# Preparing an SSM's tables with 32 products and expanded input matrices, and turning x inside two weight units

## What is computed

```
u, sq, sk, sv, dq, dk, dv, gate_logits = split(rmsnorm(x) @ w_in[l])
lam_bar = exp(lam * dt);  b_bar = ((lam_bar - 1) / lam) * bmat          # 32 groups, 64 states, 16 channels
states  = scan(lam_bar, b_bar @ u);  y = Re(c @ states) + d_skip * u
y_ssm = glu(gelu(y));  y_sb = stick_breaking(sq, sk, sv)
y_da  = rmsnorm(differential(rope(dq), rope(dk), dv), diff_subln)
x += (sum_n sigmoid(gate_n) * (branch_n @ w_branch_n)) @ w_out
x += cross_attention(rmsnorm(x), rmsnorm(mem)) @ w_xo
x += square(relu(rmsnorm(x) @ w_up)) @ w_down
```

## Time and profile before

| | |
|---|---|
| median of 3 runs (lowest to highest) | 1056.09 us (1056.09 to 1057.02) |
| the profiled execution | 1055.7 us, span 1054.0 us |
| mean granted clock | 0.988 |
| PE / DVE / ACT busy | 96% / 73% / 53% of the span |
| HBM traffic | 166 GB/s over the span |

### The profile page before, as it was taken

How to read it: one execution, slowest core, us unless ns; L and a number is a source line. 1 busy time by engine, 2 the same in 40 slices (tenths; PEclk the granted TensorE clock), 3 DMA queues, 4 the chain that set the end, 5 groups by cost and what they waited for, 6 DMA issues and landing times. The chain is left out here.

```text
span 1054.0 us, 19160 instructions
## 1 busy us (share of the span) xinstructions
PE 1009.7 (96%) x7544; PEld 895.4 (85%) x7544; DVE 765.8 (73%) x1176; ACT 563.0 (53%) x879; POOL 45.1 (4%) x100
## 2 busy tenths in 40 slices
PE   6979999999999999999989999999999989999996
PEld 6967899989897888888889779998998878888885
DVE  5958997788865766888845559877787658656664
ACT  7456535467555645444454554354657556444443
POOL 5001100000000004000000030000000000000000
PEclk9989999999999999999989999999999999999999
DMA  8625436545543555656535643364555435556561
GB/s 331 196 90 141 137 119 207 196 141 180 183 158 120 188 194 180 190 190 187 192 102 177 169 156 121 121 193 128 179 181 162 151 128 180 190 190 189 191 188 72
DMA packets 58281, 176.22 MB, mean 167 GB/s; under 512 B 14416, under 2 KB 16464, under 8 KB 58064
## 3 DMA queue, kind: packets, MB, share of 16 engines
q1 hardware_dynamic: 58048, 174.99, 52.0%
q10 hardware_dynamic: 144, 0.00, 0.0%
HBM read 171.82 MB, written 3.15 MB: 166 GB/s over the span
## 5 line engine op out<-in xcount | busy, mean ns | idle before, releaser
L1241 DVE TENSOR_TENSOR s_w_lo<-s_raw,s_w_hi 128x1024 fp32r<-128x1024 f32 x312 | 375.3, 1231 | 92.0 <-ACT s_w_hi L865 88.3
L865 ACT ACTIVATE s_w_hi<-s_raw 128x1024 fp32r<-128x1024 f32 x312 | 319.8, 1053 | 174.4 <-PE p_T L1800 73.0
L1798 PE MATMUL p_T<-s_hT,s_w_hi 128*128 128x256 f32 x576 | 166.1, 288 | 1.1 <-issue 0.6
L1799 PE MATMUL p_T<-s_hT,s_w_hi 128*128 128x256 f32 x576 | 162.9, 283 | 0.0
L1800 PE MATMUL p_T<-s_hT,s_w_lo 128*128 128x256 f32 x576 | 162.9, 283 | 0.0
L1798 PE MATMUL p_A<-s_w_hi,s_bT_hi 128*128 128x512 f32 x320 | 125.1, 391 | 2.3 <-DVE s_bT_lo L1241 2.3
L1800 PE MATMUL p_A<-s_w_hi,s_bT_lo 128*128 128x512 f32 x320 | 124.8, 390 | 0.0
L1799 PE MATMUL p_A<-s_w_lo,s_bT_hi 128*128 128x512 f32 x320 | 124.6, 389 | 0.0
L1798 PEld LDWEIGHTS p_T<-s_hT,s_w_hi 128*128 128x128 f32 x576 | 110.3, 191 | 5.2 <-issue 2.7
L1799 PEld LDWEIGHTS p_T<-s_hT,s_w_hi 128*128 128x128 f32 x576 | 110.4, 192 | 0.1
L1800 PEld LDWEIGHTS p_T<-s_hT,s_w_lo 128*128 128x128 f32 x576 | 110.3, 192 | 0.0
(11 more groups left out here) (268 smaller groups left out, 1906.8 us busy)
## 6 DMA issues: line engine op xcount, KB each, us to landing
s_raw<-in_weights SPq DMA_DIRECT2D x312, 512.0 KB, 3.5
s_x<-in_x SPq DMA_DIRECT2D x1, 1024.0 KB, 10.6
s_dv<-in_ssm_bc SPq DMA_DIRECT2D x2, 512.0 KB, 8.9
u_turn<-s_st_y SPq DMA_DIRECT2D x4, 256.0 KB, 4.9
s_uB<-u_turn SPq DMA_DIRECT2D x16, 64.0 KB, 4.0
s_bt<-in_mem SPq DMA_DIRECT2D x1, 1024.0 KB, 7.0
s_mem_t<-in_mem_t SPq DMA_DIRECT2D x1, 1024.0 KB, 9.0
y_turn<-s_st_y SPq DMA_DIRECT2D x16, 64.0 KB, 2.2
```

Of the source, the lines that this page charges most:

```text
L865: return nc.scalar.activation(o, i, f, **kw)
L1241: return V.tensor_tensor(o, i0, i1, op)
L1798: mm(o, lhi, rhi, start=first, stop=False, **kw)
L1799: mm(o, lhi, rlo, start=False, stop=False, **kw)
```

## The change

The tables are made in another way. `bN0` becomes block-diagonal over the two groups of a tile, so `mm_k` is 32 matmuls of 128 rows by 32 columns into one bank; DVE takes them out with two operations (`p_k`), adds `diag_d` there, and SP spreads them by way of DRAM into `kt` (4 + 8 DMAs, `spread_k`). `bt` is loaded already expanded by channel (`load_b`, 1 MB per layer, a new input), the powers are transposed by two small matmuls (`mm_f`), copied by ACT (`p_f`), sent through DRAM into `bF` (2 + 8 DMAs, `turn_f`), and DVE multiplies the two in place in six operations (`p_bt`); `mm_bt`, `p_bv` and their copies are gone. `p_ph` moves to units 7 and 8, `p_bt` takes units 9 to 11; `da_o` 0, `da_c` 1 and `da_n` 1 move from unit 25 to 26. The two turns of x for the MLP move into the middle of units 45 and 46, and ACT and DVE take the norm in two parts; both prepare weights early from unit 44 on. `xa_p` takes the first half of memory for all four heads and then the second. Several inputs of units are awaited by halves. In `p_b0`, `diag_d` shrinks from two operations of 64 x 512 to one of 128 x 64, with four tiny ones once. In side stages, `t` is the layer whose tables are made.

```diff
-MIDWAY = []
+K_AT = [22, 25]
+F_AT = [15, 18, 2 * (AT_UNIT["up", 0, 0] + 13) + 11, 2 * (AT_UNIT["up", 0, 0] + 13) + 14]
+MIDWAY = [("turn_x", "mlp", 0), ("turn_x", "mlp", 1)]
...
-        after(-1, "mm_bt", 1, 0)
...
-        for r in range(2):
-            after(u["bv"][r], "p_bv", tgt, r)
+        after(u["f"][0], "mm_f", tgt)
+        after(u["f"][1], "p_f", tgt)
+        for n in range(3):
+            after(u["bt"][n], "p_bt", tgt, n)
...
-        pre(0, dict(ct=-1, cv=(3, 4), b0=5, bv=(7, 8), ph=(9, 10, 11)))
-        blocks((6, 6, 7), ((9, 9), (9, 9), (10, 10), (10, 10)))
+        pre(0, dict(ct=-1, f=(2, 3), cv=(3, 4), b0=5, ph=(7, 7, 8), bt=(9, 10, 11)))
+        after(6, "mm_k", 0)
+        after(7, "p_k", 0)
...
-        pre(1, dict(ct=up0 + 12, cv=(up0 + 13, up0 + 16), b0=up0 + 17, bv=(up0 + 20, up0 + 21),
-                    ph=(up0 + 24, up0 + 25, up0 + 28)))
+        pre(1, dict(ct=up0 + 9, f=(up0 + 13, up0 + 13), cv=(up0 + 12, up0 + 13), b0=up0 + 16,
+                    ph=(up0 + 17, up0 + 20, up0 + 21), bt=(up0 + 24, up0 + 25, up0 + 28)))
     else:
-        blocks((None, 0, 1), ((None, 0), (3, 3), (4, 4), (5, 5)))
+        after(0, "p_k", 1)
...
-    after(25, "da_o", 0)
-    after(25, "da_c", 1)
-    after(25, "da_n", 1)
+    after(26, "da_o", 0)
+    after(26, "da_c", 1)
+    after(26, "da_n", 1)
     after(27, "da_o", 1)
...
     after(AT_UNIT["xo", 0], "stats", "mlp", 0)
-    after(AT_UNIT["xo", 1], "turn_x", "mlp", 0)
+    after(AT_UNIT["xo", 0], "turn_x", "mlp", 0)
+    after(AT_UNIT["xo", 0], "norm", "mlp", 0)
     after(AT_UNIT["xo", 1], "turn_x", "mlp", 1)
-    after(AT_UNIT["xo", 1], "norm", "mlp")
+    after(AT_UNIT["xo", 1], "norm", "mlp", 1)
     after(AT_UNIT["xo", 1], "stats", "mlp", 1)
...
-ACT_PREP_EARLY = set(range(0, 16)) | set(range(AT_UNIT["up", 0, 0], NU))
-DVE_PREP_EARLY = set(range(0, 6)) | set(range(AT_UNIT["up", 0, 0], NU))
+ACT_PREP_EARLY = set(range(0, 16)) | set(range(AT_UNIT["xo", 0], NU))
+DVE_PREP_EARLY = set(range(0, 6)) | set(range(AT_UNIT["xo", 0], NU))
...
+            def load_b(t):
+                load(bt[:, :, :, :], a["ssm_bt"][t], bt_landed)
+
+            def turn_f(t, part, st):
+
+                if part == 0:
+                    sp.wait_ge(*st.at(*freed(0, "X0", ("mm_f", t))))
...
+                        load(dst[r], fT[PC * r:PC * r + PC, :], f_out)
+                else:
+                    sp.wait_ge(*st.at(f_out, 2 * (t + 1)))
+                    src = f_turn[t].rearrange("(n k) (h s) -> h n k s", n=BL, h=2)
+                    for h in range(2):
+                        for j in range(BL):
+                            p = PC * h + GC * j
+                            load(bF[p:p + GC].rearrange("p r (i s) -> p (r i) s", s=STATES),
+                                 src[h, j].unsqueeze(0).broadcast_to([GC, 2 * STILES, STATES]), f_in)
+
+            def spread_k(l, part, st):
+
+                if part == 0:
+                    use = ("mm_k", l)
+                    sp.wait_ge(*st.at(*freed(l, stage_banks(use)[0], use)))
+                    dst = k_turn[l].rearrange("p (m q) n -> q p m n", q=4)
+                    for q in range(4):
+                        load(dst[q], kst[32 * q:32 * q + 32, :, :], k_out)
+                else:
+                    sp.wait_ge(*st.at(k_out, 4))
+                    for h in range(2):
+                        for j in range(BL):
+                            p = PC * h + GC * j
+                            load(kt[p:p + GC, :, GC * j:PC], k_turn[l][GC * h:GC * h + GC, :, 0:PC - GC * j], k_in)
...
+                    if l == 0 and c in F_AT:
+                        turn_f(F_AT.index(c) // 2, F_AT.index(c) % 2, st)
+                    if c in K_AT:
+                        spread_k(l, K_AT.index(c), st)
...
+                        for h in range(2):
+                            rows, c = slice(PC * h, PC * h + PC), slice(GC * h, GC * h + GC)
+                            tt(bN0[rows, r, :, c].unsqueeze(1), q[0][rows], q[1][rows], ALU.add if r else ALU.subtract)\
+                                .then_inc(*st.mid())
...
+                def p_k(t):
+
+                    use = ("mm_k", t)
+                    b = stage_banks(use)[0]
+                    src = bank[b][:, 0:BL * PC].rearrange("p (m c) -> p m c", c=PC)
+                    dve.wait_ge(*st.at(*full_at(l, b, use)))
+                    V.tensor_copy(kst[:, :, GC:PC], src[:, :, GC:PC]).then_inc(*st.mid())
+                    tt(kst[:, :, 0:GC], src[:, :, 0:GC], diag_d, ALU.add).then_inc(*st.sig(*freed(l, b, use)))
+
+                def p_bt(t, n):
+
+                    if n == 0:
+                        dve.wait_ge(*st.at(bt_landed, t + 1))
+                        dve.wait_ge(*st.at(f_in, 2 * BL * (t + 1)))
+                        for i in range(2):
+                            tt(st_y[:, i, :], bT[:, i], bF[:, i]).then_inc(*st.mid())
+                    elif n == 1:
+                        for i in range(2):
+                            tt(bF[:, 1 - i], bT[:, i], bF[:, 1 - i]).then_inc(*st.mid())
+                    else:
+                        tt(bT[:, 0], st_y[:, 0, :], st_y[:, 1, :], ALU.subtract).then_inc(*st.mid())
+                        tt(bT[:, 1], bF[:, 0], bF[:, 1], ALU.add).then_inc(*st.sig(bt_ready))
...
-                def inputs(key):
+                def inputs(key, half):
 
                     if key == ("glu", 1):
-                        return [(gelu_ready, 2)]
+                        return [(gelu_ready, half + 1)]
...
-                        return [(glu_ready, 2)]
-                    if key == ("wout", 0):
-                        return [(mg_ready, 2)]
-                    if key == ("wout", 1):
-                        return [(mg_ready, 4)]
+                        return [(glu_ready, half + 1)]
+                    if key in (("wout", 0), ("wout", 1)):
+                        return [(mg_ready, 2 * key[1] + half + 1)]
...
-                        return [freed(l, stage_banks(("xa_p", h))[0], ("xa_p", h)) for h in (2, 3)]
+                        return [freed(l, stage_banks(("xa_p", h))[0], ("xa_p", h)) for h in (2 * half, 2 * half + 1)]
                     if key[0] == "down" and key[2] == 0:
-                        return [(hid_ready, 2 * key[1] + 2)]
+                        return [(hid_ready, 2 * key[1] + half + 1)]
...
+                    elif kind == "mm_f":
+                        t = s[1]
+                        pe.wait_ge(*st.at(pow_ready, t + 1))
+                        pe.wait_ge(*st.at(*before(l, "X0", s)))
+                        for r, rows in enumerate(HALVES):
+                            ins = mm(bank["X0"][rows, 0:P], FACTORS[:, r, 3:3 + BL, :].rearrange("p n i -> p (n i)"),
+                                     ident[:, :], start=True, stop=True, skip_group_check=True)
+                        ins.then_inc(*st.sig(full["X0"]))
                     elif kind == "mm_k":
                         t = s[1]
+                        b = stage_banks(s)[0]
                         pe.wait_ge(*st.at(ct_ready, 2 * (t + 1)))
                         pe.wait_ge(*st.at(b0_ready, t + 1))
-                        for b in stage_banks(s):
-                            pe.wait_ge(*st.at(*before(l, b, s)))
-                        tiles = [(bank[b][32 * q:32 * q + 32, :], rows, q)
-                                 for b, rows in zip(stage_banks(s), HALVES) for q in range(4)]
-                        for m in range(STILES // 4):
+                        pe.wait_ge(*st.at(*before(l, b, s)))
+                        for m in range(BL):
                             for r in range(2):
-                                for o, rows, q in tiles:
-                                    mm(o[:, PC * m:PC * m + PC], bN0[rows, r, 4 * m + q, GC:3 * GC],
-                                       ct[rows, r, 4 * m + q, :], start=(r == 0), stop=False, skip_group_check=True)
...
+                                for q in range(4):
+                                    ins = mm(bank[b][32 * q:32 * q + 32, PC * m:PC * m + PC], bN0[:, r, 4 * m + q, :],
+                                             ct[:, r, 4 * m + q, :], start=(r == 0), stop=(r == 1), skip_group_check=True)
                         ins.then_inc(*st.sig(full[b]))
...
-                    elif kind == "xa_p":
...
-                        pe.wait_ge(*st.at(*before(l, b, s)))
+                    elif kind == "xa_p" and s[1] == 0:
                         for mt in range(2):
-                            ins = mm(bank[b][:, 0:T], vN[:, mt, h * P:h * P + P], eT_b[h][:, mt, :],
-                                     start=(mt == 0), stop=(mt == 1))
-                        ins.then_inc(*st.sig(full[b]))
+                            pe.wait_ge(*st.at(*freed(l, f"T{mt}", ("xv", 0))))
+                            for h in range(XA_HEADS):
+                                b, tb = stage_banks(("xa_p", h))[0], stage_banks(("xa_t", h))[0]
+                                if mt == 0:
```

(55 more changed lines are left out.)

81 lines of the change are left out of this document (27 added, 54 removed).

## The result

The changed kernel takes 1060.34 us (median of 6 runs, 1058.96 to 1062.59), the kernel before in the same session 1056.45 us. The ratio is 1.0034 with a 95% interval of 1.0022 to 1.0045: slower by 0.34%, outside the range that was forecast, and on the other side. The profiled span grew from 1054.0 to 1059.1 us, so 5.1 us are to be explained.

A forecast was written before the change was run, and what follows sets the result against it. PE, busy 96% of the span, was taken to bound the kernel, its idle time paid again through low clock. Terms summed to -7.8 us: 1047.9 against the profiled 1055.7, 1048.3 against the median; range 1038 to 1056.

The forecast's parts named there:

- Behind unit 26 a chain starts: Units 26 to 28: moved ACT and DVE stages take 9.65 us, `da_o` 1 waits 3.1; +5.14 a layer, +10.3 in all.
- rival C: Behind unit 26: two more ACT table loads of 1.28 us on the chain, +2.56 a layer, 1053.4 us; chance 0.11.
- At nothing: Loads and DMAs of `load_b`, `spread_k`, `turn_f`, and half-wise waits at branch, wout and down: no cost where PE doesn't wait.
- DVE in layer 0: Layer 0's table units: 2.1 us of new PE stalls at `sb_u` behind `nl`, 0.6 of an old wait gone; +1.5.
- Rival D: Layer 0, units 7 to 13: DVE becomes the bound and the stretch doesn't shrink, 1058.3 us; chance 0.08.
- mm_k: Layer 0 behind unit 6: 64 records take 2.0 us, saving 5.9; unit 7's low clock gives 0.7 back; -6.6.
- Start of layer 1: Before unit 0: it starts at 533.8 behind DVE's sum of x, -7.4, less 1.4 for low clock; -6.0.
- mm_bt: Its runs between units disappear: -4.2 us in layer 0, -3.5 in layer 1.
- xa_p: Before unit 44: products start at V's first half, unit 44 needs only heads 0 and 1; -2.0 a layer, -4.1 both.
- The turn: Turn for the MLP, units 45 and 46: 0.9 more work plus 1.3 for low clock; +2.2 a layer, +4.3.
- Rival B: No low clock in any of the short idle stretches: 7.7 us less, 1040.6 us; chance 0.15.
- Rival A: Behind unit 26: the moved `da_o` costs nothing, chain 7.3, clock holds; 4.6 less a layer, 1039 us; chance 0.12.

The follow-up runs named there:

- tables: Changed kernel with ACT's table sets asked for before its waits, one set for both ln and exp: 1048.00 us, ratio 0.992 to the kernel before.
- da25: Changed kernel with `da_o` 0, `da_c` 1 and `da_n` 1 put back behind unit 25: 1039.41 us, ratio 0.9833 to the kernel before.
- b_da26: Kernel before with only `da_o` 0, `da_c` 1 and `da_n` 1 moved from behind unit 25 to 26: 1077.59 us, ratio 1.0192.
- frows: Changed kernel with `f_turn` laid out so each partition of `bF` reads one 8 KB run, not 32 of 256 bytes: 1054.81 us, ratio 0.998.
- x_ph: Changed kernel with da25 and frows in it and layer 0's first four phase-table steps behind unit 6, not 7: 1033.68 us, ratio 0.9777.
- x_ph_oldxa: x_ph with `xa_p` in the old order, head by head with both memory halves in a row: 1035.74 us, ratio 0.9796 to the kernel before.

## Why the prediction was wrong, step by step

**The step that failed first** is "Behind unit 26 a chain starts", the 9.65 us. All its rows were of before, where this chain runs with the norm's functions loaded. It left out three loads of 1.28 us in each layer. They were rival C, at a chance of 0.11, with two loads and 2.56 us; the run `tables` shows 4.0 us. The remainder was sized well: from unit 26's end (215.26) to the norm's end (228.80) pass 13.54 us, which is 9.65 and three loads within 0.1; without loads PE waits 3.4 us, the forecast said 3.1. Unit 28's low clock came to 0.9 and 1.5 us (1.3 forecast). The term was +10.3 and measured +17.1; da25 and b_da26 both confirm that the placement alone makes it. From the end of unit 26 to the start of unit 28 the miss is 3.9 us a layer, the three loads. The rest is unit 26's clock, which the term left as before at 7.26 us: it took 6.02 in layer 0 and 7.50 in layer 1.

**The second** is "At nothing", the sentence on `turn_f`'s DMAs. It asked whether PE waits at that place, which it doesn't in before, and not how long the queue is held. For `spread_k` it counted the issue time from `u_turn`'s row; for `turn_f`'s 1 MB in 256-byte pieces it counted nothing. It cost 6.2 us in layer 0's units 66 and 67, and less in other versions (2.8 in da25); frows shows that the packets make it.

**The third** is "DVE in layer 0": 2.1 us of stalls forecast. One gap was 4.7 us wider than a bare one and unit 10 1.2 us longer. The place (`sb_u` behind `nl`) and the kind (DVE's table work ahead of it) were right; the size missed that five of six phase steps stand together behind unit 7, 5.9 us, so units 8 to 25 gained nothing and lost 1.4. It was not that DVE is full: x_ph has the same work, one unit earlier, and loses only the 1.2 us ahead of unit 12; with it units 8 to 25 are 3.3 us shorter than before, where 2.7 were forecast. Rival D is refuted.

**mm_k** was right in kind and priced high. It starts 0.5 us later behind unit 6 than before (it waits 1.60 where it waited 1.09), but the 64 records run in 1.10 us, not 2.0, and unit 7's clock came back whole:

```profile
54.63 1.10 PE L1978 MATMUL p_A<-s_ct,s_bN 128*32 128x64 f32 x64 [1.60 <-issue]
```

That is 17 ns a record, between the two rows that were weighed (11.6 and 32), and below the 25 ns that the prediction worked out from the Trainium skill (TensorEngine Tiling (Array Packing), Instruction Overhead). The loop writes to four column tiles in turn; no run here shows what one tile alone would take. 0.8 of the -9.0 lies in the loading phase up to unit 3 and changes from run to run (the gap there is 0.74 here and 1.07 in da25).

**Start of layer 1**: the limiter named, DVE's sum of x, was right. The charge of 1.4 for a low clock was wrong, unit 0 ran at 1.00. **mm_bt** of layer 1: -3.7 by unit 6, as forecast (3.5). **xa_p** gave 1.2, not 2.0: the products start at 330.17 as forecast and end at 333.8, but the split of the heads takes 1.26 from there, so unit 44 starts at 335.04. DVE's four parts of the split, and the first matmul of unit 44:

```profile
333.10 1.80 DVE L1263 TENSOR_TENSOR s_bT_lo<-p_A,s_bT_hi 128x256 fp32r<-128x256 f32 x4 [3.88 <-ACT s_bT_hi L906]
```

```profile
335.04 0.47 PE L1844 MATMUL p_A<-s_w_hi,s_bT_hi 128*128 128x512 f32 x1 [1.26 <-DVE s_bT_lo L1263]
```

Unit 44 starts 0.14 us after the fourth part. The half-wise wait gained nothing because heads 0 and 1 are not all that its first half needs, as the prediction had it: `unit_banks` gives unit 44 the banks A2 and A3, in which `stage_banks` puts heads 3 and 2, and PE may not write there before these are split. **The turn**: 0.8 to 0.9 a layer; the 1.3 for a low clock did not come. Rival B, no low clock, held at three of its places (unit 7, unit 0 of layer 1, unit 46) and failed at `da_o` 1. Its premise, that the wait of 2.29 ahead of unit 26 "was enough" for a low clock, is no rule: in da25 the same wait stands there, and unit 26 takes 5.99 us in both layers. Rival A, with 4.6 us less a layer, doesn't come out of its own terms: 9.65 less 7.3 and the 1.3 for the clock are 3.7.

## What to carry to other kernels

When an activation is moved across one of another table set, count the loads at its new place, and whether each comes after the engine's wait; a row of the old place has the right duration of the work and none of this. A DMA that "nobody waits for" has to be priced by its number of packets, since everything behind it on the queue waits. And a stage moved to a free-looking unit must be held against the next value that PE needs from that engine, not against the engine's share of busy time.

## What the hardware showed unexpectedly

Reading 1 MB from DRAM in 256-byte pieces brought the queue, weights included, to 112 GB/s, while with 8 KB runs the same stretch moved 252. And the granted clock after an idle stretch is no fixed price. In the changed kernel a gap of 3.0 us stands ahead of unit 26 in both layers, and the unit runs once at 1.00 and once at 0.77:

```profile
209.24:215.26 6.02, 6.02 (x50) 6.02 (x51) 3.51 (x4) 0.85 (x1) 0.00 (x0) 1.00 0.29 90
728.58:736.08 7.50, 7.50 (x50) 7.50 (x51) 3.50 (x4) 0.84 (x1) 0.00 (x0) 0.77 0.24 72
```

After the 1.9 us hole in unit 46 the clock stayed at 1.00; only in one version (x_ph_oldxa, layer 1) the same unit was at 0.83 and 1.5 us longer:

```profile
843.34:853.66 10.32, 8.43 (x42) 7.24 (x41) 7.45 (x15) 5.80 (x14) 0.00 (x0) 0.83 0.38 103
```

What decides between the two was not tried and stays open. So a low clock in a forecast is a chance and not a term: the 1.5 us come or not, with the same code and the same gap.
